# A gated recurrence and windowed attention interleaved with the projections of a two-layer model

## The reference, cut to what matters

```python
h = rms_norm(x, g_mix)
q, k, v, x_gate, x_rec = split(h @ w_in)        # 1024, 256, 256, 1024, 1024 columns
q, k = rope(q), rope(k)                         # 16 query heads, 4 key heads of 64
y_attn = windowed_gqa_sink(q, k, v, sink)       # window 128 to each side
c = centred_depthwise_conv(x_rec, conv_w, conv_b)
# for each direction, 16 blocks of 64 channels:
r = sigmoid(c @ w_a + b_a); i = sigmoid(c @ w_x + b_x)
log_a = -8 * r * softplus(-lam); a = exp(log_a)
u = sqrt(-expm1(2 * log_a)) * (i * c)
h_t = a_t * h_{t-1} + u_t                       # forward, and backward
y_lru = gelu(x_gate) * (h_fwd + h_bwd)
y = concat(rms_norm(y_attn, g_attn), rms_norm(y_lru, g_lru))
x = x + y @ w_out                               # 2048 x 2048
x = x + peer(rms_norm(x, g_ffn), ...)
```

## Time and profile before

| what | value |
|---|---|
| median of 3 runs | 3709.67 us |
| the profiled execution | 3712.13 us, span 3710.4 us |
| TensorE busy | 3385.9 us, 91% of the span |
| VectorE busy | 2242.5 us, 60% |
| ScalarE busy | 1649.5 us, 44% |
| GpSimd busy | 710.8 us, 19% |
| mean granted TensorE clock | 0.954 |
| DMA | 656.45 MB, 177 GB/s over the span |

### The profile page before, as it was taken

How to read it: one execution, slowest core, us unless ns; L and a number is a source line. 1 busy time by engine, 2 the same in 40 slices (tenths; PEclk the granted TensorE clock), 3 DMA queues, 4 the chain that set the end, 5 groups by cost and what they waited for, 6 DMA issues and landing times.

```text
span 3710.4 us, 71135 instructions
## 1 busy us (share of the span) xinstructions
PE 3385.9 (91%) x24282; PEld 3056.7 (82%) x24282; DVE 2242.5 (60%) x3607; ACT 1649.5 (44%) x2237; POOL 710.8 (19%) x648
## 2 busy tenths in 40 slices
PE   7973899999999999999999969999997979998986
PEld 6963799999988998899877859997775869978975
DVE  4544548547777777777777753335564876544454
ACT  4444445533454334433444536664333444334443
POOL 1300006940111001100000118871112111100010
PEclk9976999999999999999999979999997989999998
DMA  6510544556687668766557825554442766754522
GB/s 196 168 42 0 186 154 152 159 187 202 213 265 237 204 208 260 246 201 201 173 166 222 266 91 180 182 173 142 140 147 78 264 233 213 247 180 142 182 85 91
DMA packets 181810, 656.45 MB, mean 177 GB/s; under 512 B 23040, under 2 KB 23184, under 8 KB 180576
## 3 DMA queue, kind: packets, MB, share of 16 engines
q1 hardware_dynamic: 149328, 545.82, 46.6%
q0 software_dynamic: 32400, 109.56, 9.4%
HBM read 653.18 MB, written 2.10 MB: 177 GB/s over the span
## 4 chain that ended last, share of the span: by engine, by line
PE 82%; DVE 6%; issue 3%; ACT 3%; POOL 2%; PEld 2%; DMA 1%; DVEq 0%; ACTq 0%; SPq 0%; POOLq 0%; PEldq 0%
PE PS L525 13%; PE PS L526 13%; PE PS L527 13%; PE PS L779 6%; PE PS L781 6%; PE PS L783 6%; PE PS L577 3%; PE PS L579 3%; PE PS L581 3%; PE PS L560 2%; PE PS L561 2%; PE PS L562 2%; PE PS L732 2%; POOL w_lo L426 2%; PE PS L933 1%
## 5 line engine op out<-in xcount | busy, mean ns | idle before, releaser
L1043 ACT ACTIVATE w_hi<-raw 128x1024 fp32r<-128x1024 f32 x1032 | 1093.4, 1060 | 1702.9 <-PE PS L527 974.1
L1435 DVE TENSOR_TENSOR w_lo<-raw,w_hi 128x1024 fp32r<-128x1024 f32 x872 | 1074.5, 1233 | 931.4 <-ACT w_hi L1043 928.2
L525 PE MATMUL PS<-xt_hi,w_hi 128*128 128x256 f32 x4608 | 1326.1, 288 | 34.1 <-DVEq L1883 8.5
L526 PE MATMUL PS<-xt_lo,w_hi 128*128 128x256 f32 x4608 | 1310.2, 284 | 0.0
L527 PE MATMUL PS<-xt_hi,w_lo 128*128 128x256 f32 x4608 | 1309.6, 284 | 0.0
L525 PEld LDWEIGHTS PS<-xt_hi,w_hi 128*128 128x128 f32 x4608 | 890.8, 193 | 46.5 <-issue 35.8
L526 PEld LDWEIGHTS PS<-xt_lo,w_hi 128*128 128x128 f32 x4608 | 891.2, 193 | 0.0
L527 PEld LDWEIGHTS PS<-xt_hi,w_lo 128*128 128x128 f32 x4608 | 890.7, 193 | 0.0
L426 POOL TENSOR_TENSOR w_lo<-raw,w_hi 128x1024 fp32r<-128x1024 f32 x160 | 402.8, 2542 | 242.5 <-ACT w_hi L1043 242.5
L779 PE MATMUL PS<-w_hi,st_hi 128*128 128x512 f32 x1024 | 402.3, 393 | 0.2
L781 PE MATMUL PS<-w_hi,st_lo 128*128 128x512 f32 x1024 | 399.2, 390 | 0.0
(11 more groups left out here) (360 smaller groups left out, 3431.8 us busy)
## 6 DMA issues: line engine op xcount, KB each, us to landing
raw<-in_u_emb SPq DMA_DIRECT2D x256, 512.0 KB, 3.6
raw<-in_v_emb SPq DMA_DIRECT2D x256, 512.0 KB, 4.3
ada<-in_ada_w POOLq DMA_DIRECT2D x240, 256.0 KB, 3.7
raw<-in_xbc SPq DMA_DIRECT2D x96, 512.0 KB, 3.5
raw<-in_z SPq DMA_DIRECT2D x80, 512.0 KB, 3.6
raw<-in_q SPq DMA_DIRECT2D x64, 512.0 KB, 3.5
raw<-in_a_out SPq DMA_DIRECT2D x64, 512.0 KB, 4.8
raw<-in_k SPq DMA_DIRECT2D x48, 512.0 KB, 4.2
```

The costliest lines, as they stand in the source:

```text
L525: pe.matmul(o, w_h, x_h, start=start, stop=False, skip_group_check=True)
L526: pe.matmul(o, w_h, x_l, start=False, stop=False, skip_group_check=True)
L1043: act.activation(w_hi[:, u, :], raw[:, u, :], ACT.Copy).then_inc(hi_done, 1)
L1435: dve.tensor_tensor(w_lo[:, u, :], raw[:, u, :], w_hi[:, u, :].bitcast(F32), ALU.subtract)\
```

## The change

- The order of the tiles becomes rec, q, kv, gate, w_out. The rows of w_out are reordered: first all 16 chunks for the left 1024 columns, then again for the right ones, with the recurrent half of the input ahead of the attention half.
- `turned_blocks` replaces the wait for all 16 chunks and the first block at rec, w_pq and the second layer's k2 and q2: it waits chunk by chunk from the ninth on.
- The gate products of the recurrence run in units of two channel chunks in PSUM banks 6 and 7, two after each of the first eight q tiles; ScalarE reads them there. The input gate is a tanh of half the argument instead of a sigmoid. Decays follow beside the other q tiles, square roots beside kv, scans beside the gate blocks.
- The attention steps lie between the eight gate blocks. The score buffer `sc` is single now. The gelu of the gate is one instruction after the last block.
- The output projection has its high and low inputs in full-size tensors `y_hi` and `y_lo`; the attention half is normed and turned after its fourth tile. Addition and squares are made per column half.
- The heads are still rotated by GpSimd: queries once they are out, then keys once kv is out.

The core of the diff:

```diff
-    ("q", 4), ("kv", 2), ("gate", 4), ("rec", 4), ("w_out", 8), ("w_pq", 8),
+    ("rec", 4), ("q", 4), ("kv", 2), ("gate", 4), ("w_out", 8), ("w_pq", 8),
...
+        GATE_UNITS = [(kind, pair) for kind in (0, 2, 1, 3) for pair in range(LC // 2)]
...
 # GpSimd
-            pool.wait_ge(sem("qkv_out"), 2)
...
+                pool.wait_ge(sem("q_out"), tt + 1)
+                rotate_queries(pool, link, tt)
+            pool.wait_ge(sem("kv_out"), 1)
+            for tt in range(TT):
+                rotate_keys(pool, link, tt)
             pool.sem_inc(sem("rope_done"), 1)
...
 # TensorE
+            def turned_blocks(name, free, before, n):
+                for h in range(2):
+                    pe.wait_ge(lo_done, 4 * FIRST_BODY[name] + h + 1)
+                    for k in range(8):
+                        pe.wait_ge(xt_lo_done, KC * n + max(8 * h + k, 8) + 1)
+                        w = slice(k * P, k * P + P)
+                        last = three(PS[:, 0, 0:S], w_hi[:, h, w], w_lo[:, h, w],
+                                     xt_hi[:, 8 * h + k, :], xt_lo[:, 8 * h + k, :],
+                                     h == 0 and k == 0, h == 1 and k == 7)
+                    last.then_inc(tile_used, 1)
...
-            pe.wait_ge(xt_lo_done, KC)
-            token_columns(0, FIRST_BODY["q"], 0, 1)
-            token_columns(0, FIRST_BODY["kv"], 4, 2)
-            pe.wait_ge(sem("qkv_out"), 2)
-            channel_blocks("gate", act_free, ACT_BLOCKS["gate"])
-            pe.wait_ge(act_free, 2 + ACT_BLOCKS["gate"] + 8)
-            channel_blocks("rec", dve_free, DVE_BLOCKS["rec"])
+            turned_blocks("rec", dve_free, DVE_BLOCKS["rec"], 0)
+            pe.wait_ge(sem("bd_loaded"), 128)
+            token_columns(0, FIRST_BODY["q"], 2, 1, after=gate_units)
+            token_columns(0, FIRST_BODY["kv"], 0, 2)
...
+            for b in range(8):
+                gate_block(b)
+                if b == 0:
+                    turn_heads()
+                if b >= 3:
+                    values(b - 3)
+                if b >= 2:
+                    turn_probs(b - 2)
+                if b >= 1:
+                    scores(b - 1)
+            values(5)
+            turn_probs(6)
+            scores(7)
+            values(6)
+            turn_probs(7)
+            pe.wait_ge(sem("lru_squared"), 1)
+            for c in range(LC):
+                last = pe.matmul(PS[:, 7, 0:S], ones, rr[:, 1, c, :], start=c == 0, stop=c == LC - 1)
+            last.then_inc(sem("lru_summed"), 1)
+            values(7)
...
+            for t in range(4):
+                out_tile(t)
+            pe.wait_ge(sem("diag_done"), 2)
+            pe.wait_ge(sem("lru_root"), 1)
...
+            last.then_inc(sem("y_turned"), 1)
+            for t in range(4, 32):
+                out_tile(t)
...
 # ScalarE
+            f = FIRST_BODY["q"] + 1
+            for i in range(16):
+                high(f + i // 4, i % 4)
+                if i < 8:
+                    gate_unit(2 * i)
+                    gate_unit(2 * i + 1)
+                else:
+                    for step in range(4 * i - 32, 4 * i - 28):
+                        decays(step)
...
+            for b in range(8):
+                gate_block(b)
...
+                if b >= 2:
+                    turned_probs(b - 2)
+                if b >= 1:
+                    probs(b - 1)
+            act.wait_ge(act_free, 2 + ACT_BLOCKS["gate"] + 8)
+            flat_gate = gateT[:, :, :].rearrange("p c s -> p (c s)")
+            act.activation(flat_gate, flat_gate, ACT.Gelu_apprx_tanh).then_inc(sem("gate_done"), 1)
+            turned_probs(6)
+            probs(7)
+            act.wait_ge(sem("y_mixed"), 1)
+            act.activation(rr[:, 1, :, :], convT[:, :, :], ACT.Square).then_inc(sem("lru_squared"), 1)
+            turned_probs(7)
...
 # VectorE
+            q_work = {9: lambda: inputs(0), 10: lambda: inputs(1), 13: lambda: decay_squares(0), 14: lambda: one_minus(0)}
...
+            kv_work = {0: lambda: decay_squares(1), 1: lambda: one_minus(1), 4: lambda: drive(0)}
...
+            gate_work = {1: lambda: scan(0), 2: lambda: drive(1), 3: lambda: scan(1), 4: both_directions}
+            for b in range(8):
+                for u in (2 * (b % 2), 2 * (b % 2) + 1):
+                    low(FIRST_BODY["gate"] + b // 2 + 1, u)
+                if b >= 1:
+                    maxima(b - 1)
+                if b >= 3:
+                    head_rows(b - 3)
+                if b in gate_work:
+                    gate_work[b]()
+            dve.wait_ge(sem("gate_done"), 1)
+            dve.tensor_tensor(convT[:, :, :], rr[:, 0, :, :], gateT[:, :, :], ALU.mult).then_inc(sem("y_mixed"), 1)
+            head_rows(5)
+            maxima(7)
+            head_rows(6)
+            dve.wait_ge(sem("lru_root"), 1)
...
+            for c in range(4):
+                recurrent_scaled(c)
+            head_rows(7)
```

More of the change, by code:

```diff
@@ L545, in channel_blocks, with token_columns @@
                         block_product(name, j, b, PS[:, b, 0:S])
-            def token_columns(tiles, body0, bank0, kpt):
+            def turned_blocks(name, free, before, n):
[8 more added lines that the diff above has]
+                    last.then_inc(tile_used, 1)
+                pe.wait_ge(free, before + 2)
+                block_product(name, 0, 1, PS[:, 1, 0:S])
+                with pe.Fori(1, NB[name]) as j:
+                    for b in range(2):
+                        pe.wait_ge(free, 2 * j + before + b + 1)
+                        block_product(name, j, b, PS[:, b, 0:S])
+            def token_columns(tiles, body0, bank0, kpt, after=None):
                 n = 16 // kpt
@@ L631, in _, with gate_unit @@
-            steps = [(tt, g) for tt in range(TT) for g in range(NKV)]
+            turned_blocks("rec", dve_free, DVE_BLOCKS["rec"], 0)
+            pe.wait_ge(sem("bd_loaded"), 128)
+            def gate_unit(n):
+                kind, pair = GATE_UNITS[n]
+                pe.wait_ge(dve_free, 2 + DVE_BLOCKS["rec"] + 2 * pair + 2)
+                if n >= 2:
+                    pe.wait_ge(sem("unit_read"), n - 1)
+                for c in range(2):
+                    last = pe.matmul(PS[:, 6 + n % 2, c * S:c * S + S], wbd[:, kind, 2 * pair + c, :],
+                                     convT[:, 2 * pair + c, :], start=True, stop=True)
+                last.then_inc(sem("unit_done"), 1)
@@ L685, in _ @@
-            pe.wait_ge(sem("lru_squared"), 1)
-            for c in range(LC):
-                last = pe.matmul(PS[:, 0, 0:S], ones, rr[:, 0, c, :], start=c == 0, stop=c == LC - 1)
-            last.then_inc(sem("lru_summed"), 1)
-            pe.wait_ge(sem("y_lru_done"), 1)
-            all_rows("w_out")
+            for t in range(4, 32):
+                out_tile(t)
             pe.wait_ge(sem("x1_done"), 1)
@@ L1176, in _, with row_squares @@
[L1176 to L1183 removed]
+            def row_squares(tt):
+                act.wait_ge(sem("attn_out"), 4 * tt + 4)
+                act.activation(y_scrap, yn[:, tt, :], ACT.Square, accum_out=stat[:, tt:tt + 1])\
+                    .then_inc(sem("y_squared"), 1)
@@ new lines, in _, with add_columns @@
+            for c in range(4):
+                recurrent_scaled(c)
+            head_rows(7)
+            for c in range(4):
+                recurrent_scaled(4 + c)
+                recurrent_low(c)
+            row_norms(2)
+            for c in range(4, LC):
+                recurrent_low(c)
+            def add_columns(tt, half):
+                x = X[:, tt, half * TILE:half * TILE + TILE]
+                dve.tensor_tensor(x, x, banks(4 * half + 2 * tt, 2), ALU.add).then_inc(sem("x_half"), 1)
@@ L1633, in _ @@
+            dve.wait_ge(tile_used, 4 * FIRST_BODY["w_out"] + 32)
+            for tt in range(TT):
+                add_columns(tt, 1)
+            dve.wait_ge(sem("x_half"), 4)
+            dve.sem_inc(sem("x1_done"), 1)
+            dve.wait_ge(sem("x_squared"), 6)
+            dve.tensor_tensor(stat[:, 0:2], stat[:, 0:2], stat[:, 14:16], ALU.add).then_inc(sem("sums_added"), 1)
             row_norms(3)
```

459 lines of the change are left out of this document (263 added, 196 removed).

## The result

The changed kernel takes 3622.13 us (median of 4 runs, 3621.23 to 3622.73), the kernel before 3710.32 (4 runs, 3708.18 to 3712.93): ratio 0.9762, 95% interval 0.9745 to 0.9779. That is 88.2 us less, where 82.5 was worked out, and 3622 against a forecast of 3627. The profiled execution took 3622.12 us with a span of 3620.4, so 90.0 us less span than before.

What follows compares the result with a forecast made beforehand. Bound: 162 us without a weight tile, between recurrent and output projections. Savings of 70.1 (to the end of the output projection), 2.7 (after it) and 9.7 (other starts) sum to 82.5: 3712.1 becomes 3629.6, median 3627 us, range 3608 to 3650.

Steps and rivals of the forecast that it cites:

- Start: First recurrent block needs only nine turned chunks, so it starts when the turning matmuls end, at 31.6 us.
- Recurrent projection: Eight channel blocks moved first: 46.1 us, plus 2.5 for convolutions and 1.9 for a half-clock start; ends at 82.0.
- Queries with the gate units: Sixteen query tiles plus gate products take 57.8 us, to 139.8; ScalarE just keeps pace, costed at nothing.
- Keys and values: Eight key/value tiles at 2.72 us take 21.8 us, to 161.6; first gate block then to 167.4.
- Rotation: GpSimd's head rotation, slowed by VectorE, ends near 180 us; TensorE idles 12.6 us before head turns, bounds 4 and 20.
- Six rounds: Gate block, values, turned probabilities and scores, six times: 63.8 us, to 258.7, with maxima and probabilities hidden.
- The rival in which the rounds aren't covered: Gate rounds: late highs and lows add 9.7 us per round, 58 over six; 3685 us, chance 0.08.
- the one in which the small matmuls keep the clock low: From 82 to 300 us, small fp32 matmuls between tiles hold TensorE at 1.2 GHz; about 3790 us, chance 0.04.
- Tail: Uncovered chain from last gate block to first output tile: 31 us, bounds 28 and 37; first output tile at 289.7.
- Output projection: 32 tiles 87.0 us, half-clock start 3.1, attention turn 3.6: 93.7 us, ending at 383.4, 70.1 earlier than before.
- The other three starts: Chunk-by-chunk starts save 1.4 us at peer queries, 2.0 at second-layer keys, 6.3 at its queries: 9.7 (7 to 11).
- Rotation hidden: GpSimd finishes inside the first gate block, so 12.6 us idle and some 3 of slow clock go; 3611 us, chance 0.10.

Runs made afterwards that it cites:

- before_turned: Kernel before the change, with only the chunk-by-chunk first blocks put in for peer queries, k2 and q2; 3707.27 us against 3713.88.
- uncovered kernel: Changed kernel with all eight gate blocks first, then head turns and attention steps without tiles between them; 3652.58 us against 3622.13.
- experiment 6: Changed kernel with the four first blocks (rec, w_pq, k2, q2) waiting again for all 16 input chunks; 3632.39 us against 3622.13.
- Experiment 1: Changed kernel with the head rotation left out, keys only copied by GpSimd; 3603.55 us against 3622.13.
- Experiment 9: Changed kernel with rotation on VectorE, tail reordered, first input product moved to the first gate round, second root behind the key/value copy; 3603.51 us against 3622.13.
- experiment 8: Changed kernel with the whole rotation on VectorE, 3612.87 us; with the tail reordered as well, 3606.92 us; against 3622.13.
- experiment 4: Changed kernel with another tail order (gelu before last probabilities, square and its sums before last values), same operations; 3615.03 us against 3622.13.
- experiments 2 and 5: Against the changed kernel: 2, keys rotated by VectorE, 3616.24 us; 5, all gate blocks first, then attention steps without tiles between, 3652.58 us.

## Why the prediction was right, step by step

The mechanism and the order of things were as forecast: the gap before the head turns, released by GpSimd (10.5 us, 8 to 18 forecast), no other over 3 us before the last gate block, clock 1.00 beside the queries, rounds of 9.6 us. The sum (82.5 of 90.0 in the span) was near partly by luck. Up to 180 us the errors of its terms (+1.6, -3.5, -0.2, +4.6 us, and a rotation that started 1.7 earlier and took 2.1 longer) nearly cancelled; behind it most made the kernel faster than forecast, 6.6 us of them in the six rounds. In order of time:

*Start: 31.6 forecast, 33.20 measured.* The wait for the last low is gone as said (9.3 us from turn to product, 12.5 before), but the turning itself starts at 23.94 and not at 21.11. The constants are asked for at the same 1.81 us in both kernels and land later. The first row is the changed kernel's ScalarE, the second that of before_turned, which has the old order:

```profile
16.04 1.28 ACT L1177 ACT_TABLE_LOAD   x1 [16.04 <-DMA pc<-in_pc]
```

```profile
13.95 1.28 ACT L1106 ACT_TABLE_LOAD   x1 [13.95 <-DMA pc<-in_pc]
```

The first turn stands at 21.1 and 21.9 in the two traces of the old order, at 22.5 to 23.9 in all ten of the new one. That speaks for the new order of first loads (means 21.5 and 23.3), and some of it is variation; it wasn't settled. The prediction had priced the loads at nothing.

*Recurrent projection: 50.4 forecast, 46.9 measured.* I had carried over 2.5 us of convolution stalls and 1.9 for a half-clock start. Neither came: from 33.2 to 80 us TensorE is busy 46.4 of 46.8 us at clock 1.00. The start follows the turns without an idle, and the convolutions beside it let every low come in time; why they cost 2.5 us in the old place and none here, the runs don't show.

*Queries with the gate units: 57.8 forecast, 57.6 measured.* No wait at all: ScalarE at 41.65 busy of 58 us keeps pace, and the small fp32 products run at clock 1.00.

*Keys and values: 21.8 forecast, 26.4 measured.* This step I had wrong. I let VectorE slow the rotation and not the rotation VectorE. VectorE beside GpSimd:

```profile
143.63 2.20 DVE L1590 TENSOR_TENSOR w_lo<-raw,w_hi 128x1024 fp32r<-128x1024 f32 x1 [1.29 <-ACT w_hi L1129]
145.75 3.38 DVE L1724 TENSOR_TENSOR convT<-aa 128x2048 f32<-128x2048 f32 x1
149.16 2.21 DVE L1590 TENSOR_TENSOR w_lo<-raw,w_hi 128x1024 fp32r<-128x1024 f32 x1
```

```profile
143.46 1.28 POOL L351 TENSOR_TENSOR qT<-qn,cw 128x512 f32<-128x512 f32 x1
144.71 2.28 POOL L352 TENSOR_TENSOR qT<-qn,cw 128x512 f32<-128x512 f32 x1
146.94 3.34 POOL L353 TENSOR_TENSOR qT<-qn,cw 128x512 f32<-128x512 f32 x1
```

A low takes 2.20 us and not 1.23, the long operation 3.38 and not 2.30. So the low of one tile came 2.5 us late (156.93 above), the tile behind it ran mostly at the lower clock and took 1.8 us more, and two others came 0.4 late together.

*Rotation: end at 180 forecast, 180.36 measured.* It started 1.7 us earlier than I had it and took 38.5 us, not 36.4. The 2.27 us that I took for a step beside an operation over 2048 columns was a row of a step beside a low; beside the long one above it took 3.34. The gap was 10.5 and not 12.6 only because TensorE came 2.5 us later to it. The Trainium skill (SBUF — State Buffer, "Who interferes with whom") calls what they share an exclusive lock, and by it I had put the rotation at 23.5 + 15.5 = 39.0 us (started at 143.6 it would end at 182.6, an idle of 15 us and not the 16 that I wrote). The trace agrees with the page better than with my milder reading: 38.5 measured, and each engine's instruction is longer by somewhat less than the other's (0.97 us on the low beside a GpSimd step of 1.28, 1.00 on the step beside a low of 1.23, 2.06 on the step beside an operation of 2.28).

*Head turns to first scores: 194.9 forecast, 192.2 measured*; the head turns took 4.7 and not 5.1, the second gate block 5.9 and not 7.8.

*Six rounds: 63.8 forecast, 57.2 measured.* The largest mis-sized term. I took scores at 2.0 and values at 2.0 "at the better clock"; at clock 1.00 the scores of a step are 1.13 us, turned probabilities 1.09, values 1.89 (less their overlap, 3.86 together). The 2.08 of scores in the kernel before was a row at the lower clock, as 2.04 in the uncovered kernel confirms. Under gate blocks nothing waits but one turn (0.65 us). The rival in which the rounds aren't covered fell, and so did the one in which the small matmuls keep the clock low.

*Tail: 31 forecast, 29.0 measured* (249.4 to 278.44), granted clock 0.74. The Trainium skill (ScalarE: Activation LUTs, "What ACT_TABLE_LOAD costs") would have added a drain of 1.38 us to each table load. The trace doesn't show one: the load starts 0.02 us behind the operation before it, and the gelu 0.01 us behind the load.

```profile
254.74 1.28 ACT L1294 ACT_TABLE_LOAD   x1
256.03 1.91 ACT L1294 ACTIVATE gateT<-gateT 128x2048 f32<-128x2048 f32 x1
```

*Output projection: 93.7 forecast, 95.9 measured; from there to the next turn 7.5 and 7.2.* The turn came 82.2 us earlier than before, where these steps had summed to 72.8.

*The other three starts: 9.7 forecast, 7.8 kept.* q2 brought 6.2 and k2 2.3, of which 0.4 went again. The 1.7 at the peer queries were given back before the first layer's experts ended (the turn at 3065.58 before stands at 2983.33, again 82.2 us apart), and experiment 6 shows the same from the other side. I read this as: a start gains only where TensorE limits the stream behind it up to the next wait. That is argued from these marks, not tested.

*Rotation hidden* was a rival at 3611. Experiment 1 leaves the rotation out instead of hiding it, which is the nearest a run comes; it takes 3603.6, 18.6 below the changed kernel and not 16, since the stall of the low and the slow clock go with the gap. Experiment 9 reaches that time with the rotation done (and the new tail).

*The range.* The bounds of the terms add to 3612 and 3653, and not to the 3608 to 3650 that were written; 3622 lies in both.

## What to carry to other kernels

Price an operation that moves by a row at the clock it will have in its new place; a row beside idle time can be twice too long. When work goes beside another engine's, write down the cost in both directions, since here GpSimd's steps delayed the lows as much as the lows delayed GpSimd. And a chain on in-order engines is worth a try in another order before anything in it is made faster: 6 us in the tail came for no more work. So did the 9 from moving the rotation off the slow engine, although VectorE was busy 22.6 of the 24 us from 138 to 162 in the changed kernel, drawn out as it was.

## What of the hardware was not expected

GpSimd and VectorE draw each other out: beside each other a 128x512 step on GpSimd went from 1.28 to between 2.15 and 3.35 us, a 128x1024 low on VectorE from 1.23 to 2.20, a 128x2048 operation from 2.29 to 3.38. The rotation is 9 us dearer to the kernel on GpSimd than on VectorE (experiment 8), although VectorE then has all the work. An idle of 3.63 us left TensorE's granted clock at its higher level (head turns 1.06 us), one of 5.92 us was followed by the lower one (1.94 us). The length of the idle doesn't decide alone, though. Behind the late low, at the same place and after the same idle, the changed kernel fell to the lower clock and the kernel of experiment 4 did not (first row and second row):

```profile
158.29 0.63 PE L592 MATMUL PS<-w_hi,xt_lo 128*128 128x512 f32 x1
```

```profile
158.18 0.39 PE L593 MATMUL PS<-w_lo,xt_hi 128*128 128x512 f32 x1
```

The idles were 2.49 and 2.50 us, both at 156.93. It fell in the traces of experiments 2 and 5 too, and not in that of 6. So the 2.8 us of experiment 9 may not come again with another 3.6 us of idle.
